# First layer norm of a decoder step: scale and shift by feature moved behind the transposes, and the loads at the start reordered

## The reference, cut to what matters

```
def layer_norm(x, g, b):
    mu = mean(x); var = mean(square(x - mu))
    return (x - mu) * rsqrt(var + EPS) * g + b        # per row; g, b by feature

h = layer_norm(x, ln_in_g, ln_in_b)
p = h @ w_in + b_in          # split into three groups of heads
...                          # attention, sparse attention, HGRN2
x = layer_norm(ALPHA * h + mixer(h)); x = layer_norm(ALPHA * x + moe(x))
```

## Time and profile before

| | us |
|---|---|
| median of 3 runs | 1399.96 (1394.69 to 1400.25) |
| profiled execution, its own time | 1398.77 |
| span of the profiled execution | 1396.9 |
| PE busy | 1262.4 (90%) |
| DVE busy | 732.2 (52%) |
| ACT busy | 413.5 (30%) |
| first matmul (strips) starts | 14.32 |
| first transpose starts | 25.86 |
| first projection starts | 56.30 |
| values of head 0 start | 101.40 |
| mean granted clock of PE | 0.952 |

### The profile page before, as it was taken

The page is one execution under the profiler, slowest core; times in us unless marked ns, Lnnn a source line. Parts: engine busy times, 40 slices in busy tenths (PEclk is TensorE's granted clock), DMA queues, the critical chain, the costliest instruction groups (busy, mean ns, idle before and its releaser), DMA issues.

```text
span 1396.9 us, 19607 instructions
## 1 busy us (share of the span) xinstructions
PE 1262.4 (90%) x6900; PEld 757.3 (54%) x6900; DVE 732.2 (52%) x1724; ACT 413.5 (30%) x877; POOL 177.4 (13%) x209
## 2 busy tenths in 40 slices
PE   3699999999999999979898999999729999999966
PEld 1468787787877645656665664445323333333322
DVE  5625585574764201378778773434653333334339
ACT  2232232331421201155666771313200111111016
POOL 0003121031131000030000000000000222211131
PEclk9699999999999999989999999999859999999988
DMA  9812011040110403033310006300366959394855
GB/s 320 245 34 61 2 51 41 18 76 0 33 61 6 127 25 61 19 103 65 100 41 1 16 16 191 130 31 31 131 227 218 356 202 328 122 349 153 278 182 222
DMA packets 124391, 163.19 MB, mean 117 GB/s; under 512 B 29891, under 2 KB 98675, under 8 KB 124312
## 3 DMA queue, kind: packets, MB, share of 16 engines
q1 hardware_dynamic: 109992, 112.75, 26.3%
q0 software_dynamic: 14320, 49.41, 10.2%
HBM read 225.01 MB, written 36.45 MB: 187 GB/s over the span
## 4 chain that ended last, share of the span: by engine, by line
PE 73%; DVE 16%; DMA 3%; issue 3%; ACT 2%; POOL 1%; SPq 0%; DVEq 0%; POOLq 0%; ACTq 0%
PE act L688 16%; PE vec L1228 11%; PE vec L988 9%; PE vec L717 7%; PE vec L738 4%; PE act L913 4%; PE vec L901 3%; DMA arena<-x_rows,arena 2%; PE act L1241 2%; PE vec L1241 2%; PE act L925 2%; PE act L938 1%; PE vec L698 1%; DVE arena L1901 1%; DVE arena L1917 1%
## 5 line engine op out<-in xcount | busy, mean ns | idle before, releaser
L688 PE MATMUL act<-arena 128*128 128x352 f32 x768 | 238.7, 467 | 0.4 <-issue 0.4
L688 PEld LDWEIGHTS act<-arena 128*128 128x128 f32 x768 | 145.5, 193 | 76.7 <-issue 3.0
L1228 PE MATMUL vec<-arena 128*64 128x512 f32 x768 | 172.5, 601 | 3.1 <-issue 3.1
L988 PE MATMUL vec<-arena 128*128 128x512 f32 (+1 forms) x288 | 128.3, 600 | 0.8 <-DVE arena L1926 0.8
L1228 PEld LDWEIGHTS vec<-arena 128*64 128x64 f32 x768 | 54.1, 138 | 104.6 <-issue 104.3
L717 PE MATMUL vec<-arena 128*128 128x512 f32 (+1 forms) x256 | 100.3, 546 | 0.0
L2214 DVE TENSOR_SCALAR arena<-arena 128x256 f32<-128x256 f32 x24 | 7.1, 296 | 171.4 <-ACT arena L1562 171.4
L988 PEld LDWEIGHTS vec<-arena 128*128 128x128 f32 (+1 forms) x288 | 51.5, 182 | 69.2 <-issue 67.2
L1471 ACT ACTIVATE arena<-arena 128x640 f32<-128x640 f32 (+15 forms) x128 | 81.3, 639 | 8.7 <-DVE arena L1901 8.4
L1901 DVE CUSTOM_DVE_ANT_0 arena<-vec,arena 128x128 f32<-128x128 f32 (+6 forms) x168 | 68.9, 430 | 25.2 <-PE vec L901 16.2
L1462 ACT COPY arena<-act 128x512 f32<-128x512 f32 (+11 forms) x176 | 63.2, 429 | 54.8 <-PE act L913 54.5
(11 more groups left out here) (379 smaller groups left out, 1928.2 us busy)
## 6 DMA issues: line engine op xcount, KB each, us to landing
arena<-in_exp_w SPq DMA_DIRECT2D x144, 1024.0 KB
y_rows<-arena POOLq DMA_DIRECT2D x48, 256.0 KB, 4.9
arena<-in_w_in SPq DMA_DIRECT2D x16, 512.0 KB, 7.1
arena<-in_x_prompt SPq DMA_DIRECT2D x8, 512.0 KB, 8.8
x_spill<-arena POOLq DMA_DIRECT2D x8, 512.0 KB, 4.4
arena<-x_spill SPq DMA_DIRECT2D x8, 512.0 KB, 5.0
arena<-in_cache_fox_kv SPq DMA_DIRECT2D x16, 256.0 KB, 3.5
x_rows<-arena POOLq DMA_DIRECT2D x8, 512.0 KB, 2.9
```

The source lines that it names most:

```text
L688: last = mm(bk[:, 0:n], W[k % 2][:, c, m * P:(m + 1) * P], xT[:, c, a:a + n], start=c == 0, stop=c == NC - 1)
L988: last = mm(bk[:r], src, Wo[half][:, c, :], start=c == 0, stop=c == NC - 1)
L1228: last = mm(gu_bank[p][o], xgT[p][:, c, o], Wgu[:, slot, c, :], start=c == 0, stop=c == NC - 1)
```

## The change

- The groups are 3, 3 and 3 tiles. DVE makes (x - mean) * root in one TENSOR_SCALAR per tile, without gain and shift. The root is a Sqrt on ACT and a reciprocal on DVE; a first Sqrt of `eps_col` loads its table ahead. The root of group 0 stands in ACT's queue behind two of the four strips, and the third root behind the evictions of group 0.
- PE transposes a group at a time: one bank holds one chunk of features for the three tiles, so features lie on partitions. ACT applies gain and shift as scale and bias (`lncol`, gain and shift by feature, [128, 8] each) while it moves groups 0 and 1, both rings, and the odd chunks of group 2 out of PSUM. DVE does the even chunks of group 2.
- PE begins with the projection pieces of head 0 when groups 0 and 1 are transposed: piece 1, the transposes of group 2, and pieces 2 to 9. Piece 3 waits for DVE's evictions.
- Gain and shift on the rows for the residual are two TENSOR_TENSORs per tile on DVE, after all three groups are normal: groups 0 and 1, then the evictions of group 2, then group 2. POOL's spills wait for them. DVE's wait for the spills moves behind `reset`, ahead of the prelude.
- SP's queue: x0 to x2, the identity alone, the gain and shift columns, x3 to x8, the biases, the weights of head 0 (each block with a semaphore of its own, the first needed one in front), the rest of the constants, the gain and shift rows, the page table and so on. The three loads for the strips go to POOL's queue, in front.

```diff
--- before.py
+++ after.py
...
-GROUPS = (range(0, 3), range(3, 7), range(7, 9))
+GROUPS = (range(0, 3), range(3, 6), range(6, 9))
...
+    lncol = zs.take(2 * NC, 2)
...
-                e.dma_start(ln_g, bcast(I["ln_in_g"], D)).then_inc(*E.moved("ln_in"))
-                e.dma_start(ln_b, bcast(I["ln_in_b"], D)).then_inc(*E.moved("ln_in"))
-                e.dma_start(consts, I["consts"]).then_inc(*E.moved("consts_in"))
...
-                e.dma_start(tab33[0:32, :], I["rel_bias_table"]).then_inc(*E.moved("tab_in"))
-                e.dma_start(tab33[32:33, :], I["masked_row"]).then_inc(*E.moved("tab_in"))
-                e.dma_start(onehot[0:33, :], I["bucket_rows"]).then_inc(*E.moved("tab_in"))
+                e.dma_start(ident, I["consts"][:, 0:P]).then_inc(*E.moved("ident_in"))
+                for n, name in enumerate(("ln_in_g", "ln_in_b")):
+                    e.dma_start(lncol[:, n, :], I[name].rearrange("(c p) -> p c", p=P), allow_slow_non_contiguous=True).then_inc(*E.moved("lncol_in"))
+        b = I["b_in"][0]
+        e.dma_start(bcol[:, 0:8], b[HQ:HQ + 1024].rearrange("(h p) -> p h", p=P), allow_slow_non_contiguous=True).then_inc(*E.moved("bcol_in"))
...
         def load_w(k):
             if k >= 2:
                 e.wait_ge(*E.at(("w_in used", k - 2)))
             dst = W_nkvg if k == 6 else W[k % 2]
-            for a, c, n in w_blocks[k]:
-                e.dma_start(dst[:, :, a:a + n], w_view[:, :, c:c + n]).then_inc(*E.moved(f"w{k % 2}_in", ("w_in", k)))
+            for a, c, n in ([w_blocks[0][x] for x in (1, 0, 2, 3)] if k == 0 else w_blocks[k]):
+                e.dma_start(dst[:, :, a:a + n], w_view[:, :, c:c + n]).then_inc(*(E.moved(f"w{k % 2}_in", ("w_in", k)) if k else E.moved(f"first{a // P}_in", ("w_in", 0, a // P))))
 
         load_w(0)
-        b = I["b_in"][0]
+        e.dma_start(consts[:, P:], I["consts"][:, P:]).then_inc(*E.moved("consts_in"))
+        e.dma_start(ln_g, bcast(I["ln_in_g"], D)).then_inc(*E.moved("ln_in"))
+        e.dma_start(ln_b, bcast(I["ln_in_b"], D)).then_inc(*E.moved("ln_in"))
...
-        e.wait_ge(*E.at("x transposed pe"))
...
-        e.wait_ge(*E.at("consts_in"))
         e.wait_ge(*E.at("tab_in"))
         for a in range(0, STRIPW, 512):
             n = min(512, STRIPW - a)
-            e.wait_ge(*E.free("act"))
             bk = E.bank("act")
             mm(bk[0:H, 0:n], tab33[:33, :], onehot[:33, a:a + n], start=True, stop=True).then_inc(*E.filled("act"))
-        for t in range(NT):
-            e.wait_ge(*E.at(("x normal", t)))
-            r = rows(t)
-            for half in range(2):
-                ring = "act" if half else "vec"
+        e.wait_ge(*E.at("ident_in"))
+
+        def turn_normal(g):
+            for t in GROUPS[g]:
+                e.wait_ge(*E.at(("x normal", t)))
+            for c in range(NC):
+                ring = "act" if c % 2 else "vec"
                 e.wait_ge(*E.free(ring))
                 bk = E.bank(ring)
-                for c in range(4):
-                    last = e.transpose(bk[:, c * P:c * P + r], X1[:r, t, (4 * half + c) * P:(4 * half + c + 1) * P], ident[:r, :r])
-                last.then_inc(*E.filled(ring, "x transposed pe"))
+                for n, t in enumerate(GROUPS[g]):
+                    r = rows(t)
+                    last = e.transpose(bk[:, n * P:n * P + r], X1[:r, t, c * P:(c + 1) * P], ident[:r, :r])
+                last.then_inc(*E.filled(ring, ("x transposed pe", g)))
 
         def project(k, m, third):
             a, n = third
-            e.wait_ge(*E.at(("w_in", k)))
+            e.wait_ge(*E.at(("w_in", k, m) if k == 0 else ("w_in", k)))
...
-        e.wait_ge(*E.at("xT by vec"))
-        e.wait_ge(*E.at("xT by act"))
-        for piece in pieces_of(0):
+        for g in range(2):
+            turn_normal(g)
+        for n, piece in enumerate(pieces_of(0)):
+            if n < 3:
+                e.wait_ge(*E.at(("xT ready", n)))
+            if n == 2:
+                e.wait_ge(*E.at("xT by vec"))
             project(*piece)
+            if n == 0:
+                turn_normal(2)
+        e.wait_ge(*E.at(("w_in", 0, 3)))
+        e.wait_ge(*E.at("consts_in"))
...
-        def rsqrt_of_variance(tag, between=lambda g: None):
-            E.stage(tag)
-            for g, tiles in enumerate(GROUPS):
-                r = rstd[:, tiles[0]:tiles[-1] + 1]
-                e.wait_ge(*E.at(("variances", tag, g)))
-                act(r, r, ACT.Ln).then_inc(*E.done())
-                e.wait_ge(*E.own())
-                act(r, r, ACT.Exp, scale=-0.5).then_inc(*E.done(("rstd", tag, g)))
-                between(g)
+        def roots(g):
+            r = rstd[:, GROUPS[g][0]:GROUPS[g][-1] + 1]
+            e.wait_ge(*E.at(("variances", "ln0", g)))
+            act(r, r, ACT.Sqrt).then_inc(*E.done(("rstd", "ln0", g)))
+
+        def turned(g, rings=("vec", "act")):
+            a, n = GROUPS[g][0] * P, sum(rows(t) for t in GROUPS[g])
+            for c in range(NC):
+                ring = "act" if c % 2 else "vec"
+                if ring in rings:
+                    e.wait_ge(*E.full(ring))
+                    bk = E.job(ring)
+                    act(xT[:, c, a:a + n], bk[:, 0:n], ACT.Identity, bias=lncol[:, 1, c:c + 1], scale=lncol[:, 0, c:c + 1]).then_inc(*E.drained(ring, ("xT ready", g)))
...
+        e.wait_ge(*E.at(("eps", 0)))
+        act(rstd[:, 0:1], eps_col, ACT.Sqrt).then_inc(*E.done("root table"))
...
+            if a == 512:
+                roots(0)
+        e.wait_ge(*E.at("lncol_in"))
+        roots(1)
+        turned(0)
+        roots(2)
+        turned(1)
+        e.wait_ge(*E.at("bcol_in"))
...
+            if n == 0:
+                turned(2, ("act",))
...
+        e.memset(mv, 1.0).then_inc(*E.done())
+        for g, tiles in enumerate(GROUPS):
+            for t in tiles:
+                r = rows(t)
+                e.wait_ge(*E.at(f"x{t}_in"))
+                for half in range(2):
+                    e.bn_stats(stats[:r, t, 6 * half:6 * half + 6], X1[:r, t, 512 * half:512 * half + 512]).then_inc(*E.done())
+            e.wait_ge(*E.own())
+            for t in tiles:
+                r = rows(t)
+                e.bn_aggr(mv[:r, t, :], stats[:r, t, :]).then_inc(*E.done())
+            e.wait_ge(*E.own())
+            if g == 0:
+                e.wait_ge(*E.at("root table"))
+            r = rstd[:, tiles[0]:tiles[-1] + 1]
+            ts(r, mv[:, tiles[0]:tiles[-1] + 1, 1], EPS, None, ALU.add).then_inc(*E.done(("variances", "ln0", g)))
+            e.wait_ge(*E.at(("rstd", "ln0", g)))
+            e.reciprocal(r, r).then_inc(*E.done())
+            e.wait_ge(*E.own())
+            for t in tiles:
+                x, r = X1[:rows(t), t, :], rows(t)
+                ts(x, x, mv[:r, t, 0:1], rstd[:r, t:t + 1], ALU.subtract, ALU.mult).then_inc(*E.done(("x normal", t)))
+        e.wait_ge(*E.at("ln_in"))
+
+        def gain_and_shift(g):
+            e.wait_ge(*E.at(("x transposed pe", g)))
+            for t in GROUPS[g]:
+                x, r = X1[:rows(t), t, :], rows(t)
+                tt(x, x, ln_g[:r], ALU.mult).then_inc(*E.done())
+                e.wait_ge(*E.own())
+                tt(x, x, ln_b[:r], ALU.add).then_inc(*E.done(("x scaled", t)))
+
+        gain_and_shift(0)
+        gain_and_shift(1)
+        a, n = GROUPS[2][0] * P, sum(rows(t) for t in GROUPS[2])
+        E.jobs["vec"] = 7
+        e.wait_ge(*E.at("lncol_in"))
+        for c in range(0, NC, 2):
+            e.wait_ge(*E.full("vec"))
+            bk = E.job("vec")
+            ts(xT[:, c, a:a + n], bk[:, 0:n], lncol[:, 0, c:c + 1], lncol[:, 1, c:c + 1], ALU.mult, ALU.add).then_inc(*E.drained("vec", "xT by vec"))
+        gain_and_shift(2)
-        e.wait_ge(*E.at("x_spill"))
...
+        e.wait_ge(*E.at("x_spill"))
...
+        e.dma_start(tab33[0:32, :], I["rel_bias_table"]).then_inc(*E.moved("tab_in"))
+        e.dma_start(tab33[32:33, :], I["masked_row"]).then_inc(*E.moved("tab_in"))
+        e.dma_start(onehot[0:33, :], I["bucket_rows"]).then_inc(*E.moved("tab_in"))
         for t in range(NT):
-            e.wait_ge(*E.at(("x normal", t)))
+            e.wait_ge(*E.at(("x scaled", t)))
```

More of the change, by code:

```diff
@@ L189, in free @@
         n, depth = self.jobs.get(ring, -1) + 1, len(self.banks[ring])
-        return self.at(("drained", ring, n - depth) if n >= depth else "consts_in")
+        return self.at(("drained", ring, n - depth) if n >= depth else "ident_in")
     def emptied(self, ring):
@@ L474, in _ @@
             if t == 2:
[L475 to L483 removed]
+                e.dma_start(ident, I["consts"][:, 0:P]).then_inc(*E.moved("ident_in"))
[3 more added lines that the diff above has]
+        e.dma_start(bcol[:, 0:8], b[HQ:HQ + 1024].rearrange("(h p) -> p h", p=P), allow_slow_non_contiguous=True).then_inc(*E.moved("bcol_in"))
+        e.dma_start(bcol[:, 8:12], b[HG:HG + 512].rearrange("(h p) -> p h", p=P), allow_slow_non_contiguous=True).then_inc(*E.moved("bcol_in"))
```

(6 more changed lines are left out.)

43 lines of the change are left out of this document (4 added, 39 removed).

## The result

The change took the kernel from a median of 1400.11 us (4 runs, 1394.69 to 1400.89) to 1377.42 us (4 runs, 1374.27 to 1379.24): ratio 0.985, 95% interval 0.9829 to 0.9871. Forecast were 1382 and a range of 1374 to 1389. The profiled execution took 1378.48 (span 1376.6, mean granted clock 0.956); 1381.7 was the sum made for it.

What follows compares the result with a forecast made beforehand. DVE's queue sets PE's third piece: rows at 31, 15.0 of gain and shift, evictions to 47.8; plus 33.1 for seven pieces and 3.4 clock gives 84.3 against 101.4. 1398.8 - 17.1 = 1381.7, say 1382; range 1374 to 1389.

Steps and rivals of the forecast that it cites:

- cost of the half clock: PE's seven pieces after its pause: slow clock adds 3.4 us, between 2.6 and 4.7.
- I take 6, since little is in flight then: Bucket table loads on POOL's queue: the table lands at 6 us, between 5 and 10.
- Rival 1: DVE's gain and shift: small pieces cost nothing, start at 27.3, 3.7 us more gained, 1378; chance 0.10.
- Rival 2: Head 0's prelude on DVE waits for late spills and gives the gain back, 1392 to 1399; chance 0.05.
- The 77 of the prediction: Head 0's prelude: spills landing after 77 us would begin to cost time.
- Rival 3: Gain-row loads: 3712 small pieces take 6.4 us rather than 2.6, rows land at 35, 1386; chance 0.13.
- the sum's price: Small DMA pieces ahead of the gain rows: 1151 took 0.8 us, so 3712 take 2.6.
- Rival 4: POOL's table loads land late and the whole norm waits, slower than before, over 1400; chance 0.03.
- point of decision at 9.7: Bucket table landing: beyond 9.7 us, each further us is a us on the path.
- Rival 5: DVE's norm: TENSOR_SCALAR with two scalar columns not fast, adds 4.7 us, only 1 past the rows; inside the forecast.
- the term of 15.0: DVE's queue ahead of the evictions: twelve gain and shift operations of 1.22 us plus six waits, to 46.0.

Runs made afterwards that it cites:

- rows_first: The change with gain and shift rows ahead of head 0's weights in SP's queue; median 1374.33 us, 0.983 of the kernel before.
- evict_first: The change with DVE's four evictions of group 2 ahead of all gain and shift work; median 1370.07 us, 0.9801 of the kernel before.
- tight: both_first with ACT draining group 1 before the third root and PE's piece 2 before group 2's transposes; median 1367.5 us, 0.9805 of before.
- both_first: The change with evictions ahead of gain and shift and the first root ahead of all strips; median 1366.59 us, 0.9791 of the kernel before.
- late_prelude: The change with 32 memsets of a free buffer on DVE after the last gain and shift; median 1391.71 us, 0.9958 of the kernel before.
- loads_alone: The kernel before with the change's load order and identity wait, without gain and shift columns; median 1403.64 us, 1.0044 of the kernel before.
- both_first_again: The same kernel as both_first, run once more on the chip of tight; 1369.96 us, 0.9816 of the kernel before.
- norm_alone: The change with SP's old load order, keeping gain columns, the identity's own load and weight-block order; median 1381.18 us, 0.9885 of the kernel before.
- root_first: The change with group 0's root ahead of all strips in ACT's queue; median 1378.24 us, 0.9869 of the kernel before.

## Why the prediction was right

The prediction's path was the path: DVE's queue from the rows over gain and shift to the evictions, then PE's third piece. Its steps against the trace:

| step | predicted | measured |
|---|---|---|
| bucket table lands | 6 (5 to 10) | 9.3 |
| root of group 0 | 10.2 | 13.4 |
| one TENSOR_SCALAR with two columns of scalars | 0.7 | 0.75 |
| DVE's norm ends | 27.3 | 29.9 |
| PE's first piece starts | 25.5 | 28.7 |
| PE's second piece ends | 38 to 44 | 42.8 |
| gain and shift rows land | 31 | 30.9 |
| twelve gain and shift operations | 15.0 | 14.4 |
| evictions end | 47.8 | 47.3 |
| cost of the half clock | 3.4 (2.6 to 4.7) | 1.6 |
| values of head 0 start, by the chain | 84.3 | 82.35 |
| shift against before | 17.1 | 19.05 |

**Three terms were mis-sized.** "I take 6, since little is in flight then" was wrong for the table: its last load took 6.8 from issue to landing, near the 7.5 of the slowest spill. SP's loads of x went at the same time, and the DMA engines were busy for 95% of the time from 4 to 6 us and for all of it from 6 to 8; that this is the cause no run shows. It made the root, the norm and the first piece some 3 us late. That this cost nothing is luck: the sum happened to have 3.7 of waiting for the rows behind it, and 0.96 was left. The clock's cost, 3.4, had been taken above the 2.6 of before because there were no transposes just ahead; it was 1.6, less than the lower end of its bounds. The seven pieces at full clock take 33.37 by `rows_first`, where the sum had 33.1. Together that makes 34.95 from piece 3 to the values instead of 36.5, so 1.55 of the 1.95 by which the front was better than the sum. The other 0.4 is piece 3's earlier start. In the third term, the twelve operations had a hop counted on top of each second 1.22, while their starts are 1.26 and 1.15 apart by turns (0.6 less), and the evictions took 2.0 instead of 1.8. The span fell by 20.3 rather than 17.1; of the 1.2 beyond the front's 19.05, 1.1 are PE's shorter waits for gathered rows near the end, as the table of shifts has it. The medians, 22.7 apart, hold 2 us more, which is within what one kernel varies by: the kernel before spread over 6 us in the 15 runs beside `evict_first`, its span between 1391.9 at a mean clock of 0.956 and 1397.8 at 0.952.

**Rival 1** (rows in time) did not come, and came near. The rows bound by 0.96. `rows_first` shows what they were worth: 0.86 at piece 3, not 3.7, since DVE's own end was at 29.9 instead of 27.3.

**Rival 2** (the gain given back in head 0) is refuted: the prelude waited 4.70 for the softplus, not for the spills, which had landed by then. Even where the spills did end the wait, in `evict_first`, `tight` and both runs of `both_first`, it was at 58 to 62, and `late_prelude` puts the limit some 22 us after 60.69, at about 82. The 77 of the prediction was on the safe side.

**Rival 3** (small pieces dear) is refuted, and the price in the sum holds. This is the 1 us from 7.5 to 8.5 of the kernel after, when the gain columns went with next to nothing beside them:

```profile
DMA packets 1630, 0.03 MB, mean 29 GB/s; under 512 B 1614, under 2 KB 1628, under 8 KB 1630
```

The DMA engines were busy all the time, so 1614 pieces took 1.0 us or a little less, 0.6 us per thousand. The sum had 0.8 for 1151 (0.7 per thousand), the rival 6.4 for 3712 (1.7). `loads_alone` says the same in the landing: it lacks the 2048 pieces of the gain columns, and its rows land at 29.55 instead of 30.89, 1.3 sooner, where the sum's price gives 1.4; from kernel to kernel this landing varies by some 0.5 (30.30 in `late_prelude`, 31.17 in `both_first_again`). The Trainium skill, "DMA: Bandwidth & Descriptors", "Specifications", says that below 512 B the DMA engine does a read-modify-write. Whether it did so here no trace shows; a small piece cost about a third of what a 512-byte row did.

**Rival 4** (POOL's queue late) has its point of decision at 9.7 by the prediction. The table came at 9.3 and DVE's norm ended 20.6 later, so measured the point is near 10.3, the rows' 30.9 less these 20.6. `norm_alone`, with the table at 14.7, is the nearest trial of what lies beyond: piece 3 at 51.74, 4.3 later for a table 5.4 later, which fits 5.4 less the 0.96 that the rows leave. The mechanism is there, though that kernel has other loads moved too; the landing did not reach it.

**Rival 5** (the two-scalar form slow) is refuted by the 0.75. The Trainium skill, "VectorE: DVE Perf Modes", "Mode 2×_2P", has fp32 operations with one tensor source from SBUF at twice the rate of those with two, and the trace agrees in direction, at a ratio of 1.6: 0.75 against 1.22 for the same 1024 columns, with both scalars read from columns.

What the prediction did not ask is whether the four evictions had to stand where they stood. It named the term of 15.0 on the path and took it as given. `evict_first` moves these twelve operations, for which PE does not wait, behind the evictions and has the values 6.2 us sooner.

## What to carry to other kernels

Follow the engine that releases the bottleneck back through its own queue, and ask of every instruction ahead of the released one who needs it and when: here 14.4 us of work for a residual that is read hundreds of us later (`x_spill`, first at 823) stood in front of the 2 us of evictions that PE waited for. Price a part only in the kernel that it will be in: nearly the same reordering of loads was worth minus 9.0 us with the old norm and plus 4.5 with the new, the early root nothing or 4.1, the early table nothing while PE waited for the whole constants as well. And where two waits end within 1 us of each other, removing one brings out the other: the rows in time were worth 0.86 at piece 3.

## What the runs showed of the hardware

The length of PE's pause does not fix the price. Two kernels had the same pause of 3.54 us after the same piece. In `rows_first` the clock stayed at 1.00; in `norm_alone` it fell, and the seven pieces took 35.07 instead of 33.37:

```profile
50.00:52.00 2.00, 0.26 (x1) 0.29 (x2) 2.00 (x5) 0.00 (x0) 0.52 (x1) 1.00 0.52 211
52.00:54.00 2.00, 2.00 (x5) 1.14 (x5) 1.97 (x3) 0.00 (x0) 0.00 (x0) 0.62 0.18 70
54.00:56.00 2.00, 2.00 (x5) 1.13 (x4) 1.97 (x3) 0.00 (x0) 0.53 (x1) 0.53 0.31 123
```

After 4.1 us in `late_prelude` the loss over the seven pieces was 1.5, after 4.6 us in the change 1.6, after 8.4 us in `root_first` 2.2 (34.88, 34.95 and 35.56 against 33.37). So a pause of this kind cost nothing, or 1.5 to 2.2 us on top of itself, and one twice as long hardly more. And the clock also fell where PE had had no pause for 20 us, at 898 us in the kernel before, and at 160 us in the change, 6 us behind a gap of 0.44 that left the kernel before at full clock.

Small pieces of a DMA cost 0.6 us per thousand here when nothing else shared the DMA engines (1614 of them, 7.5 to 8.5 us in the change).
